# Two blocks of two layers on one core: layer loops written out, loads for the next layer issued ahead, gate and residual in the experts' sum, part of the condition product on the PE

## What is computed

```python
def first_block(x, c, ...):
    cond = silu(c)                                   # 1024
    for l in range(DEPTH):
        mod = cond @ w_ada[l] + b_ada[l]             # 1024 x 6144
        shift1, scale1, gate1, shift2, scale2, gate2 = split(mod, 6)
        h = x * (1 + scale1) + shift1
        y = token_mixer(h, w_in[l], ...)             # attention, spatial gating, gates, w_out
        x = layer_norm(ALPHA * x + gate1 * y, ln1_g[l], ln1_b[l])
        h = x * (1 + scale2) + shift2
        y = moe_ffn(h, ...)                          # top 8 of 64 experts, FF 256, and a shared one
        x = layer_norm(ALPHA * x + gate2 * y, ln2_g[l], ln2_b[l])

def second_block(x, ...):
    for l in range(DEPTH):
        x = x + 0.5 * swiglu(rms_norm(x, norm_ffn1[l]), ffn1_in[l], ffn1_out[l])
        x = x + mixer(rms_norm(x, norm_mix[l]), ...) # RWKV-7 in two directions, differential attention
        x = x + 0.5 * swiglu(rms_norm(x, norm_ffn2[l]), ffn2_in[l], ffn2_out[l])
```

## Time and profile before

| | us |
|---|---|
| median of 3 runs | 3982.89 |
| lowest, highest | 3978.73, 3984.99 |
| the profiled execution | 3978.22 |
| its span, first to last instruction | 3976.5 |
| PE busy | 3405.7 |
| DVE busy | 1562.6 |
| ACT busy | 843.5 |
| POOL busy | 603.5 |
| mean granted clock of PE, share of full | 0.909 |

### The profile page before, as it was taken

One profiled execution on the slowest core, in us unless ns is written; L12 is line 12 of the kernel. 1 busy time (PEld: TensorE's weight loads), 2 busy tenths in 40 slices (PEclk: granted clock), 3 DMA queues, 4 the chain that ended last, 5 costly groups with the idle time before them and its releaser, 6 DMA issues.

```text
span 3976.5 us, 46296 instructions
## 1 busy us (share of the span) xinstructions
PE 3405.7 (86%) x18496; PEld 2349.6 (59%) x18496; DVE 1562.6 (39%) x2703; ACT 843.5 (21%) x1240; POOL 603.5 (15%) x556
## 2 busy tenths in 40 slices
PE   6878999993888799999199978787979997878799
PEld 3755334331566334333098658775978965868498
DVE  4433222224533222222454255543535425644354
ACT  1211111110130111111133232111324213111132
POOL 5402233331440233333000000000000000000000
PEclk8979999996878899999599988898999998889899
DMA  7646999995753899999554310003536422000442
GB/s 271 228 172 249 387 388 387 388 378 184 274 184 148 336 385 383 379 382 362 201 187 143 111 54 1 22 36 124 191 118 217 159 82 83 1 22 1 159 169 96
DMA packets 305420, 799.38 MB, mean 201 GB/s; under 512 B 57030, under 2 KB 155868, under 8 KB 251308
## 3 DMA queue, kind: packets, MB, share of 16 engines
q1 hardware_dynamic: 245804, 727.16, 48.4%
q0 software_dynamic: 58848, 67.05, 5.1%
q10 hardware_dynamic: 544, 2.10, 0.1%
HBM read 989.01 MB, written 53.48 MB: 262 GB/s over the span
## 4 chain that ended last, share of the span: by engine, by line
PE 41%; DVE 7%; ACT 1%; issue 1%; DMA 1%; SPq 0%; DVEq 0%
PE s_bank L1929 13%; PE s_bank L1967 6%; PE s_bank L1903 3%; PE s_bank L1916 3%; PE s_bank L2114 2%; PE s_bank L1994 2%; PE s_bank L2129 2%; PE s_bank L2225 2%; PE s_bank L2124 2%; PE s_bank L2235 1%; PE s_bank L2102 1%; DMA s_ringA<-in_ffn_in 1%; PE s_bank L2191 1%; PE s_bank L2025 0%; PE s_bank L2200 0%
## 5 line engine op out<-in xcount | busy, mean ns | idle before, releaser
L711 PE MATMUL f_bank<-f_ringA,f_arena 128*64 128x512 f32 x3072 | 689.8, 602 | 25.0 <-DMA f_ringA<-in_w_up,f_chosen 17.8
L711 PEld LDWEIGHTS f_bank<-f_ringA,f_arena 128*64 128x64 f32 x3072 | 216.5, 138 | 416.4 <-issue 415.2
L1929 PE MATMUL s_bank<-s_hT_high_parts,s_highA_parts 128*128 128x256 f32 x1408 | 402.1, 286 | 17.7 <-DVE s_hT_parts L2461 17.7
L1929 PE MATMUL s_bank<-s_hT_parts,s_highA_parts 128*128 128x256 f32 x1408 | 401.7, 285 | 0.0
L1929 PE MATMUL s_bank<-s_hT_high_parts,s_ringA_parts 128*128 128x256 f32 x1408 | 401.4, 285 | 0.0
L732 PE MATMUL f_bank<-f_ringB,f_arena 128*64 128x512 f32 x1536 | 346.1, 592 | 1.0 <-DVE f_arena L1475 1.0
L1012 ACT ACTIVATE f_arena<-f_bank 128x512 f32<-128x512 f32 (+1 forms) x362 | 202.0, 587 | 575.3 <-PE f_bank L692 174.1
L1467 DVE TENSOR_TENSOR f_arena<-f_arena,f_bank 128x256 f32<-128x256 f32 x96 | 58.6, 610 | 600.3 <-ACT f_arena L1090 600.3
L1929 PEld LDWEIGHTS s_bank<-s_hT_high_parts,s_highA_parts 128*128 128x128 f32 x1408 | 273.6, 194 | 20.4 <-issue 19.0
L1929 PEld LDWEIGHTS s_bank<-s_hT_parts,s_highA_parts 128*128 128x128 f32 x1408 | 273.6, 194 | 1.4
L1929 PEld LDWEIGHTS s_bank<-s_hT_high_parts,s_ringA_parts 128*128 128x128 f32 x1408 | 273.6, 194 | 0.0
(11 more groups left out here) (398 smaller groups left out, 5565.5 us busy)
## 6 DMA issues: line engine op xcount, KB each, us to landing
f_ringA<-in_w_gate SPq DMA_DIRECT2D x128, 1024.0 KB, 8.8
f_ringA<-in_w_up SPq DMA_DIRECT2D x128, 1024.0 KB, 11.6
f_ringB<-in_w_down SPq DMA_DIRECT2D x128, 1024.0 KB, 12.6
s_ringA<-in_ffn_in SPq DMA_DIRECT2D x88, 1024.0 KB, 7.6
f_ringA<-in_w_ada SPq DMA_DIRECT2D x48, 1024.0 KB, 8.6
s_arena<-in_ffn_out SPq DMA_DIRECT2D x44, 1024.0 KB, 6.1
s_ringA<-in_w_in SPq DMA_DIRECT2D x40, 1024.0 KB, 6.8
f_ringA<-in_w_in SPq DMA_DIRECT2D x28, 1024.0 KB, 10.3
```

Of the source, the lines that this page charges most:

```text
L711: last = mm(ps[j * CAP:(j + 1) * CAP, :].rearrange("p (h c) -> p h c", h=2), picked[:, b % 2, k, j * CAP:(j + 1) * CAP], gu[j][:, :, k, :] ...
L1929: last = mm(ps[:, t * S:(t + 1) * S], parts_of(wx[:, k, cs_]), parts_of(hx[:, k, :]), start=(k == 0 and x == 0), stop=(k == DT - 1 and x = ...
```

## The change

1. The layer loops are written out in Python, each layer has a plan of banks of its own, and waits for register values become constants. `leave` adds one `nop`. Some semaphores move to the outer program (`kept`); block 2's are cleared in parts.
2. The first third of the condition product (chunks 0 to 3) goes from DVE's sums to PE: per chunk eight products whose stationary side is `cond`, one column broadcast to 32, and whose moving side is 512 columns of weights, into 32 partitions of one bank. ACT copies the bank, PE turns it in four pieces, DVE adds the bias (`take_early`).
3. This early product is done for layer 1 at the end of layer 0. SP loads chunk 0 when the last up product is done, chunk 1 after six y loads, chunks 2 and 3 after the eighth; chunk 3 goes to the arena. The rows of both layers are loaded once, at the start.
4. At the end of layer 1 of block 1, and of layer 0 of block 2, SP loads the next layer's first three up weights (`up_ahead`) in the same way; `s_ringA` takes the address of `f_ringA`.
5. The y rows come back into six places (slot 3 of ringA and ringB) instead of eight. The seventh and eighth load wait for DVE's first two sums.
6. Gate and residual move. DVE multiplies both halves of a down product by `gate_b`, ahead of the copy of the turned hidden, and ACT copies none. At pair 2 `begin_sum` multiplies `y_sum` by the gate and adds ALPHA times x. The final `residual` goes, `norm_x` reads `y_sum`.
7. In block 2, ACT takes the root before it splits the first up weights.

```diff
-            with sp.Fori(0, DEPTH) as l:
+            for l in range(DEPTH):
+                banks = layer_banks[l]
...
+                def early_ada(l, c):
+
+                    dst = ada_place(l, c)
+                    src = a["w_ada"][l, :, c * 512:(c + 1) * 512].rearrange("(k p) c -> p k c", p=P)
+                    for h in range(2):
+                        sp.dma_start(dst[:, h * 4:(h + 1) * 4], src[:, h * 4:(h + 1) * 4]).then_inc(ada_landed[c], 16)
...
+                def ahead(n):
+
+                    if l + 1 < DEPTH:
+                        early_ada(l + 1, n)
+                    elif n < 3:
+                        up_ahead(n)
+
                 banks.read(sp, ("up", PAIRS - 1))
-                sp.wait_ge(y_room, PAIRS - 2)
+                ahead(0)
+                sp.wait_ge(y_room, 1)
...
+                    if i == len(y_back):
+                        ahead(1)
+                    if i >= len(y_back):
+                        sp.wait_ge(y_summed, i - len(y_back) + 1)
+                    sp.dma_start(y_back[i % len(y_back)], y_of[:, m, k * D:(k + 2) * D]).then_inc(y_landed[i], 16)
+                for n in (2, 3):
+                    ahead(n)
...
+            def early_ada(l):
+
+                ps = banks.claim(pe, ("ada rows", l))
+                for c in range(third):
+                    pe.wait_ge(ada_landed[c], 32 * l + 32)
+                    w = ada_place(l, c)
+                    for k in range(DT):
+                        last = mm(ps[32 * c:32 * c + 32, :], cond[:, k:k + 1].broadcast_to([P, 32]), w[:, k, :],
+                                  start=(k == 0), stop=(k == DT - 1))
...
+                banks.fill(last, ("ada rows", l))
+                banks.evacuated(pe, ("ada rows", l))
...
+                for t in range(4):
+                    last = turn(ps[:, t * P:(t + 1) * P], ada_rows[:, t * P:(t + 1) * P], ident[:, :])
...
+                if l + 1 < DEPTH:
+                    early_ada(l + 1)
                 leave(pe, l)
...
+                def begin_sum():
+
+                    for m in range(MT):
...
+                        last = tt(y_sum[:, m, :], y_sum[:, m, :], gate_b[:, :], ALU.mult)
+                    step(last)
+                    for m in range(MT):
+                        last = v.scalar_tensor_tensor(y_sum[:, m, :], x_tok[:, m, :], ALPHA, y_sum[:, m, :],
+                                                      ALU.mult, ALU.add)
...
+                    if b:
+                        for n in range(2):
+                            key = ("down", b - 1, n)
+                            ps = banks.read(dve, key)
+                            banks.free(tt(y_tok[:, (b - 1) % 3, n, :], ps[:, :], gate_b[:, n * 512:(n + 1) * 512],
+                                          ALU.mult), key)
...
-                norm_x(4, ln2_landed, 2)
+                norm_x(4, ln2_landed, 2, y_sum)
+                if l + 1 < DEPTH:
+                    take_early(l + 1)
...
+                if l + 1 < DEPTH:
+                    for s in range(slots_A):
+                        n = max(i for i in range(len(slot_of)) if slot_of[i] == s)
+                        banks.read(sp, last_use[n])
+                        up_ahead(l + 1, s)
...
                 last.then_inc(squares_ready, 1)
+                roots(MT)
                 if k != 1:
                     split_up(k, 0)
-                roots(MT)
```

More of the change, by code:

```diff
@@ L359, in first_block @@
-        for g in range(2):
-            banks.take(("gate2", g), g)
-        banks.take(("g", "shared"), 4)
-        banks.take("places", 6)
-        banks.take(("u", "shared"), 5)
-        for b in range(2):
-            banks.take(("row", b), 2 + b % 2)
-        banks.take("turned", 7)
-        banks.take("before", 6)
-        banks.take("spill", 7)
-        for n in range(4):
-            banks.take(("y", n), n)
-        for b in range(2, AHEAD):
-            banks.take(("row", b), 2 + b % 2)
@@ L383, in spills @@
+        layer_banks = [plan(l) for l in range(DEPTH)]
         def spills(b):
@@ L550, in _ @@
         def _(pool):
-            with pool.Fori(0, DEPTH) as l:
+            for l in range(DEPTH):
+                banks = layer_banks[l]
                 def param(dst, src):
@@ L1109, in _ @@
             v.memset(one[:, :], 1.0)
-            with dve.Fori(0, DEPTH) as l:
+            for l in range(DEPTH):
+                banks = layer_banks[l]
                 step = Chain(dve, dve_steps)
@@ L1739, in second_block @@
+            for m in range(MT):
+                banks.take(("gate", m), 6 + m)
+            for g in range(2):
+                banks.take(("oaT", g), 4 + g)
+            for t in range(DT):
+                banks.take(("branch", t), t % 4)
+            for n in range(2):
+                for m in range(MT):
+                    banks.take(("out", n, m), 4 + 2 * n + m)
+            take_ffn(2)
+            return banks
+        layer_banks = [plan() for l in range(DEPTH)]
         a_at = STEPS
@@ L1773, in leave @@
             eng.wait_ge(s_go, l + 1)
+            eng.nop().then_inc(left, 1)
         @block.sync
         def _(sp):
-            with sp.Fori(0, DEPTH) as l:
+            for l in range(DEPTH):
+                banks = layer_banks[l]
                 def slot_free(n):
@@ L1976, in ffn @@
                             last.then_inc(down_done, 1)
-            with pe.Fori(0, DEPTH) as l:
+            for l in range(DEPTH):
+                banks = layer_banks[l]
                 ffn(0, l)
```

534 lines of the change are left out of this document (299 added, 235 removed).

## The result

The changed kernel takes 3917.05 us (median of 4 runs, 3913.83 to 3918.06) against 3983.94 for the kernel before (4 runs): a ratio of 0.983, 95% interval 0.982 to 0.985, or 66.9 us less where 53 were forecast. The profiled execution took 3917.83 us, 60.4 less than the one before.

The account below looks back on a forecast made before the run. PE, 86% busy, was taken as the bound, leaving its waits at layer ends; +5.1-25.7-0.3-18.1-14.3=-53.3 us from the profiled 3978.22 gives 3924.9, and with the median 4.67 above it 3930, range 3912 to 3985.

Parts of the forecast that it names:

- What bounds it: Whole kernel: PE is busy 86% of the span, so only shorter PE work or PE's waits at layer ends can pay.
- rival E: Between the blocks: the wait on leaving block 1 shrinks too, by 8 us, giving 3922; chance 0.04.
- case A: Main case: the clock rises under the early product and the gaps shrink, -53.3 us in sum, 3930; chance 0.48.
- Start of layer 0: Up to the first projection: PE's 32 products replace DVE's four sums, +5.1 us if the clock rises.
- Rival B: Early product in both layers: the clock stays low under the 32-column products, sum -8.2 us, 3975; chance 0.33.
- Rival C: Early product in both layers: low clock plus weight loads in front of each record, +13.9 us, 3997; chance 0.07.
- Rival D: Boundary and block 2's loads: transfers collide, chunks 1 to 3 land 10 to 15 us late, 3945 to 3955; chance 0.08.
- Boundary: Block 1, last down product to layer 1's first projection: loading ahead and the early product save 25.7 us.
- End of block 1 and first chain: Into block 2: residual and later y loads -0.3, root first with weights already there -18.1; leaving the block unchanged.
- Second chain: Start of block 2's layer 1: same reordering and loads ahead -12.4, back edge 2 more, -14.3 us in all.
- The experts' loop: Gates delay the copy of the turned hidden: 0.35 us per layer, last pair only, rounded away; begin_sum hides.
- The back edges: Layer ends: written-out loops nearly remove SP's 4.1 and ACT's 3.2 us; the 9.1 us between blocks is not covered.

Follow-up runs that it names:

- x_onegroup: Changed kernel with a bank and four small adding products per chunk, but all early products in one column group; 3951.23 us.
- x_fold: Changed kernel with each chunk's eight early products spread over four column groups, added up by four small products; 3921.55 us (0.9853).
- x_nogate: Changed kernel with gate and residual back behind the experts' sum and ACT copying the first down half again; 3925.90 us (0.9859).
- x_after: The changed kernel itself, run and profiled once more as the base for the follow-up runs; 3918.82 us (0.9843 to the kernel before).
- x_merged: Changed kernel with both blocks' programs in one program block, only the layer's barrier between them; 3911.36 us (0.9824).
- x_fold2: Changed kernel with early products over four column groups and ACT copying the first two chunks' banks ahead of the norm's root; 3912.75 us (0.9826).
- x_inahead: Changed kernel with the first projection's first weights of layer 1 also loaded at the end of layer 0; 3911.00 us (0.9829).

## Why the prediction was right, and where not

**What bounds it**: right. Three of the four gaps moved, by -16.6 to -29.0 us, and made the gain; the fourth, the start of layer 0, did not move beyond scatter, nor did the bodies.

**The number.** The gaps gave 66.6 us where 53.3 were forecast, and the bodies took 5.9 back where no change was. So the profiled execution came out at 3917.83 us for 3924.9, 7.1 of the 13 between 3930 and 3917.05. The other 5.9 are scatter and rounding: I had put the median 4.67 above the profiled execution, and it lay 0.8 below. 3917 is in fact nearer to rival E's 3922 than to my 3930, but E's mechanism did not happen (the exit's 8.9 us stayed); the chain of case A did, with terms that were too large.

**Start of layer 0**, forecast +5.1, measured -0.6. DVE's sums went and the product on PE took their place, but three terms of its price were off. The product, 29.8 with its ramp, took 23.86, since I added up products that run beside one another; chunk 0 landed at 21.46, not 22.8: 7.3 us too many. The ramp of 1.6 that I credited to L790 was not saved: behind 2.8 us of waiting the clock was down again, and the projection took 1.0 us longer than before. Counted to the projection's end the place cost 0.4 to 1.2 us where 5.1 were forecast.

**Rival B**, 33% on a low clock, is refuted by the windows: 0.99 and 1.00 under the 32-column products. The row with 64 rows at 0.50 that I leaned on the earlier trace rows was 3.4 us long, about as long as the projection itself ran at 0.50 (some 3.1 us before, 5 after). **Rival C** fell with `x_onegroup`: 7.05 us for sixteen records leave no room for a weight load. The rule of the Trainium skill (TensorE: Matmul & The Clock Gate, Part 3: Packing small matmuls), that a weight load overlaps only where the row group differs, and the 0.197 us of the earlier trace rows would have made it 10.2 (8.8 with the 0.110 that these narrow loads take): the trace speaks against it for this form. The same part says that products in different tiles of the array run at the same time; I had read it for the loads only, and `x_fold` shows it, 1.92 against 7.05 us.

**Rival D**, loads that collide, is refuted as well. Counted from the last down product, which ended 2.2 us later than before, chunks 1 and 2 reached PE at 27.4 and 38.2 us where 26.9 and 37.3 were forecast, not 10 to 15 late.

**Boundary**, forecast -25.7, measured -29.0. PE's product last and the norm hidden was right, and `x_nogate` shows it: 6 us more of norm did not lengthen it. DVE's sum ended 35.2 us after the last down product for 34.6. (My 5.4 us a chunk and 2.5 us a y load are quicker than the 373 GB/s that I read, which give 5.6 and 2.8; the windows from 940 and 960 us had 426 and 387 GB/s, so it did little harm.) Of the 3.2 that were off, 1.3 lie ahead of SP's first issue, 0.7 of them the barrier (0.3 for 1.0), and 1.9 behind it: the first weights came 12.64 us after their issue for 14.55. "This stretch needs weights first, then nothing else" was wrong: the projection starts earlier than its later weights arrive, and part is given back further on, 3.05 us here, 0.52 in `x_after`, whose first wait was longer (12.34 us for 10.61). To the projection's end the boundary gained 26.9 to 27.5. PE's timeline of the changed kernel:

```profile
1029.44 14.00 PE L872 MATMUL f_bank<-f_ringA,f_hT 128*128 128x512 f32 x32 [3.05 <-DMA f_ringA<-in_w_in]
```

**End of block 1 and first chain**, forecast -18.4, measured -20.35. The exit stayed (8.9 for 9.1), as said, though for a reason that only `x_merged` showed. That the residual's 5.8 us and the later y loads cancel was right too: the norm ends 45.67 us after the last down product, 45.65 before. The table load of 1.28 us went, which I had not seen. PE's turns began at 1935.01, 2.7 us behind x, since the rows landed late: so turns and DVE's split end together, not the split alone.

**Second chain**, forecast -14.3, measured -16.6: 12.7 of it behind the first square, as forecast (12.4); 3.9 ahead of it for 2, as the back edge shrank to 0.6 us with its table load.

**The experts' loop**: the last pair's wait before L732 grew from 0.52 to 1.06 us, for 0.35. The bodies' +2.8, +1.3, +2.3 and -0.5 us are within what two profiles of one kernel differ by. The first projections account for +1.0 of the first and +2.1 of the second; what is left is not explained.

**The back edges.** The written-out loops took 4.1 to 0.3 and 3.2 to 0.6 us. That agrees with the Trainium skill's rule (Runtime: NRT & Kernel Launch, Instruction fetch mechanics); no run kept loops and dropped the register waits, so the fetch itself is argued, not shown. The exit was no branch of that kind in my reading, and yet merging the blocks took it to 0.33.

## What to carry to other kernels

Price a gap by what stands in it, in order, and ask what is late next: here loading ahead was worth 15+24 us, while the move of sums to another engine by itself and the residual taken out of a hidden place gave next to nothing. Small products with a narrow stationary side belong in different column groups, four at a time, spread within one chunk, not over chunks. After a gap has been closed, look at the next transfer behind it, which was covered by the old wait, and count the gap to the end of the stage behind it: of the 5.0 and 8.4 us that `x_fold2` and `x_inahead` took off the boundary, at most 1.0 and 5.1 were left by then.

## What the runs showed of the hardware

- fp32 products of 128 rows by 32 columns by 512: sixteen records in 7.05 us in one column group, in 1.92 us over four.
- PE's granted clock was 0.99 to 1.00 under such products, and 0.50 again at 49.54 us, behind waits of 0.78 and 2.80 us with 0.63 us of work between them; three idle products in the second wait held it at 1.00, worth 2.6 us in the projection behind.
- Leaving a program block and entering the next cost 8.9 us, a barrier inside one block 0.3.
- At the end of a layer SP issued its first load 4.1 us behind DVE's last step with hardware loops and 0.3 with the loops written out.
- With layer loops written out, ACT did not load its table (1.28 us) ahead of the squares; with hardware loops it did in both layers.
